# An expert's scatter at the end of the next expert, and each expert's count read at its own branch

## The reference

```python
def _moe_swiglu(h, w_router, b_router, w_gate, w_up, w_down):
    ...
    gates = jnp.einsum("tk,tke->te", top_w,
                       jax.nn.one_hot(top_idx, N_EXPERTS, dtype=jnp.float32))
    out = jnp.zeros((bsz * s, d), jnp.float32)
    for e in range(N_EXPERTS):
        y_e = _swiglu(tok, w_gate[e], w_up[e], w_down[e]).astype(jnp.float32)
        out = out + gates[:, e:e + 1] * y_e
    return out.astype(h.dtype).reshape(bsz, s, d)
```

## Time and profile before

| | us |
|---|---|
| median of 3 runs | 1776.54 (1773.34 to 1780.08) |
| profiled execution, its own time | 1776.94 |
| span of that execution's trace | 1775.1 |
| experts, first product of e0 to last product of e7 (from the timeline) | 837.85 to 1761.4 |
| PE busy over the span | 1599.4 (90%) |
| DMA, mean over the span | 274 GB/s, 403 to 409 GB/s in its fullest slices |

### The profile page before, as it was taken

The page is one execution under the profiler, slowest core; times in us unless marked ns, Lnnn a source line. Parts: engine busy times, 40 slices in busy tenths (PEclk is TensorE's granted clock), DMA queues, the critical chain, the costliest instruction groups (busy, mean ns, idle before and its releaser), DMA issues.

```text
span 1775.1 us, 24622 instructions
## 1 busy us (share of the span) xinstructions
PE 1599.4 (90%) x10871; PEld 912.8 (51%) x10872; DVE 371.6 (21%) x782; ACT 217.9 (12%) x416; POOL 101.7 (6%) x131
## 2 busy tenths in 40 slices
PE   7967899999999999997989999979979979887875
PEld 5633467777578866546343343345645653423322
DVE  1669320000055533403011001011011011110101
ACT  1411120000041133302000000000000000000001
POOL 5036200000000011100000000000000000000000
PEclk8988899999999999997999999999989989999999
DMA  9444576554384412332999977999969979999996
GB/s 330 150 147 167 189 279 250 220 218 150 113 311 143 143 48 75 116 142 96 382 403 409 362 290 267 404 408 408 403 250 347 388 266 397 403 409 404 409 408 248
DMA packets 167300, 485.81 MB, mean 274 GB/s; under 512 B 12928, under 2 KB 15872, under 8 KB 167168
## 3 DMA queue, kind: packets, MB, share of 16 engines
q1 hardware_dynamic: 157328, 481.51, 71.3%
q10 hardware_dynamic: 9840, 2.33, 0.7%
HBM read 482.78 MB, written 1.05 MB: 273 GB/s over the span
## 4 chain that ended last, share of the span: by engine, by line
PE 72%; DMA 11%; DVE 6%; issue 5%; SPq 2%; ACTq 1%; ACT 1%; POOL 0%; DVEq 0%
PE bank L1659 22%; PE bank L1209 20%; PE bank L1690 10%; DMA ring<-in_moe_w_down 8%; PE bank L1393 4%; PE bank L1584 3%; PE bank L1503 3%; DMA ring<-in_moe_w_up 3%; SPq L424 2%; PE bank L1636 2%; ACTq L530 1%; PE bank L1234 1%; DVE arena L921 1%; DVE arena L929 1%; PE bank L1542 1%
## 5 line engine op out<-in xcount | busy, mean ns | idle before, releaser
L1659 PE MATMUL bank<-ring,arena 128*32 128x256 f32 (+3 forms) x4864 | 510.0, 430 | 73.6 <-issue 46.6
L1659 PEld LDWEIGHTS bank<-ring,arena 128*32 128x32 f32 (+1 forms) x4864 | 230.1, 122 | 342.3 <-issue 267.7
L1209 PE MATMUL bank<-arena,ring 128*128 128x256 f32 x1280 | 287.0, 384 | 1.3 <-ACT arena L641 1.0
L1690 PE MATMUL bank<-ring,arena 128*32 128x256 f32 (+1 forms) x2128 | 253.2, 464 | 26.9 <-DMA ring<-in_moe_w_down 26.8
L1209 PEld LDWEIGHTS bank<-arena,ring 128*128 128x128 f32 x1280 | 243.9, 193 | 39.1 <-issue 4.5
L1690 PEld LDWEIGHTS bank<-ring,arena 128*32 128x32 f32 (+1 forms) x2128 | 103.1, 121 | 166.6 <-issue 119.6
L1134 DVE TENSOR_TENSOR arena<-arena,bank 128x512 f32<-128x512 f32 (+2 forms) x44 | 24.4, 576 | 607.8 <-PE bank L1659 607.8
L750 ACT ACTIVATE arena<-bank 128x512 f32<-128x512 f32 (+2 forms) x44 | 21.1, 508 | 696.7 <-PE bank L1671 576.4
L1393 PE MATMUL bank<-ring,arena 128*128 128x512 f32 x176 | 77.0, 595 | 0.3 <-PE bank L1209 0.3
L1234 PE MATMUL bank<-ring,cT 128*32 128x512 f32 x384 | 54.7, 695 | 8.9 <-ACT cT L583 8.3
L1503 PE MATMUL bank<-ring,arena 128*128 128x512 f32 x128 | 57.7, 593 | 0.3 <-PE bank L1209 0.3
(11 more groups left out here) (266 smaller groups left out, 1157.1 us busy)
## 6 DMA issues: line engine op xcount, KB each, us to landing
ring<-in_moe_w_gate SPq DMA_DIRECT2D x56, 2048.0 KB, 16.9
ring<-in_moe_w_up SPq DMA_DIRECT2D x56, 2048.0 KB, 16.8
ring<-in_moe_w_down SPq DMA_DIRECT2D x56, 2048.0 KB, 18.5
ring<-in_ada_w SPq DMA_DIRECT2D x24, 2048.0 KB, 9.1
ring<-in_m_w_in SPq DMA_DIRECT2D x12, 2048.0 KB, 9.1
ring<-in_ffn_w_gate SPq DMA_DIRECT2D x5, 2048.0 KB, 17.7
ring<-in_ffn_w_up SPq DMA_DIRECT2D x5, 2048.0 KB, 11.9
ring<-in_ffn_w_down SPq DMA_DIRECT2D x5, 2048.0 KB, 9.1
```

The lines of the kernel that those rows point to most:

```text
L1209: ins = mm(out_, l, r, start=i == 0, stop=i == len(pairs) - 1, **kw)
L1659: ins = mm(ps[base + b // per][m * h:m * h + m, w * (b % per):w * (b % per) + w], hcur3[:, kc, m * b:m * b + m], sl[:, kc - half * rows, w ...
L1690: ins = mm(ps[4 + b // per][m * h:m * h + m, w * (b % per):w * (b % per) + w], actT[:, t % 2, b // per, n * (b % per) + i, m * q:m * q + m ...
```

## The change

An expert's scatter moves. In experts 1 to 6 PE now runs `scatter(e-1)` as the very last thing of expert e's copy, right ahead of the jump or compare that leads to e+1. It writes banks 6, 7, 2, 3 instead of 6, 7, 4, 5 (`SCATTER_LATE`). DVE adds its result at the start of expert e+1, and PE waits for that before the first up tile of e+1. The last expert, e7, does it as before for e6: the scatter of e6 stands behind e7's first gate, with the old banks. Since y_sb of e-1 now lives until the end of e, ACT and DVE wait for `scat_mm` before they overwrite it, and there are three gate buffers instead of two (the third is part of `hd`).

`gather(0, 0)` and the eight idle products behind it move into e0's branch. Each engine loads an expert's count right ahead of that expert's branch, one load at each of eight places, instead of nine loads ahead of e0; the overflow flag is loaded at the end.

```diff
-        gates_of = (dtw.rearrange("p a b -> p (a b)"), area(3840, TOK))
+        gates_of = (dtw.rearrange("p a b -> p (a b)"), area(3840, TOK),
+                    hd.rearrange("p a b c -> p (a b c)")[:, 0:TOK])
...
-        SCATTER = (6, 7, 4, 5)
+        SCATTER, SCATTER_LATE = (6, 7, 4, 5), (6, 7, 2, 3)
...
                 act.wait_ge(s["tile_used"], k * ITEM + (MOE0 + ITEM))
+                past(act, "scat_mm", k * 4)
                 for dst, src in output_parts(nb, m, 0):
...
             def take_outputs(k, nb, m):
                 dve.wait_ge(s["tile_used"], k * ITEM + (MOE0 + ITEM))
+                past(dve, "scat_mm", k * 4)
...
             def item(e, nb, m):
 
-                if e:
-                    add_outputs(e - 1)
+                if e == NE - 1:
+                    add_outputs(e - 2, SCATTER_LATE)
+                    add_outputs(e - 1, SCATTER)
+                elif e >= 2:
+                    add_outputs(e - 2, SCATTER_LATE)
...
-                    take_gates(e + 1, gates_of[(e + 1) % 2], e)
+                    take_gates(e + 1, gates_of[(e + 1) % 3], max(e - 1, 0))
...
             gather(0, 0)
-            sizes = [count_of(dve, i) for i in range(NE)]
+            for e in range(NE):
+                sized(dve, count_of(dve, e), lambda nb, m: item(e, nb, m))
+            add_outputs(NE - 1, SCATTER)
             over = count_of(dve, 2 * NE)
-            for e in range(NE):
-                sized(dve, sizes[e], lambda nb, m: item(e, nb, m))
-            add_outputs(NE - 1)
...
             def item(e, nb, m):
-                expert(e, e, nb, m, lambda: scatter(e - 1, gates_of[(e - 1) % 2]) if e else None,
-                       lambda: gather(e + 1, e + 1) if e + 1 < NE else None)
+                last = e == NE - 1
+
+                def after_gate():
+                    past(pe, "acc_done", max(e - 1, 0) * 4)
+                    if last:
+                        scatter(e - 1, gates_of[(e - 1) % 3], SCATTER)
+
+                if e == 0:
+                    gather(0, 0)
+                    stay_warm(WARM_ITEM, 2)
+                expert(e, e, nb, m, e if last else max(e - 1, 0), after_gate,
+                       lambda: None if last else gather(e + 1, e + 1))
+                if e and not last:
+                    past(pe, "gT_ready", e + 2)
+                    scatter(e - 1, gates_of[(e - 1) % 3], SCATTER_LATE)
...
-            gather(0, 0)
-            stay_warm(WARM_ITEM, 2)
-            sizes = [count_of(pe, i) for i in range(NE)]
+            for e in range(NE):
+                sized(pe, count_of(pe, e), lambda nb, m: item(e, nb, m))
+            scatter(NE - 1, gates_of[(NE - 1) % 3], SCATTER)
             over = count_of(pe, 2 * NE)
-            for e in range(NE):
-                sized(pe, sizes[e], lambda nb, m: item(e, nb, m))
-            scatter(NE - 1, gates_of[(NE - 1) % 2])
```

More of the change, by code:

```diff
@@ L759, in _ @@
             first_counts(act, "act")
-            sizes = [count_of(act, i) for i in range(NE)]
+            for e in range(NE):
+                sized(act, count_of(act, e), lambda nb, m: item(e, e, nb, m))
             over = count_of(act, 2 * NE)
-            for e in range(NE):
-                sized(act, sizes[e], lambda nb, m: item(e, e, nb, m))
             items = overflow(act, "act", over, lambda: None, lambda g, k: item(g, k, 2, 64), lambda g, k: None)
@@ L1122, in take_tokens, with take_gates @@
                 ins.then_inc(s["hg_ready"], 1)
-            def take_gates(n, gates, k):
+            def take_gates(n, gates, scattered):
                 past(dve, "gT_mm", n + 1)
-                past(dve, "scat_mm", k * 4)
+                past(dve, "scat_mm", scattered * 4)
                 v.tensor_copy(gates, ps[3][:, 0:TOK]).then_inc(s["gT_ready"], 1)
@@ L1141, in take_outputs, with add_outputs @@
                 ins.then_inc(s["y_high"], 1)
-            def add_outputs(k):
+            def add_outputs(k, banks):
                 past(dve, "acc_done", k * 4)
@@ L1147, in add_outputs @@
                     past(dve, "scat_mm", k * 4 + i + 1)
-                    tt(o, o, ps[SCATTER[i]][:, :], ALU.add).then_inc(s["acc_done"], 1)
+                    tt(o, o, ps[banks[i]][:, :], ALU.add).then_inc(s["acc_done"], 1)
             def item(e, nb, m):
-                if e:
-                    add_outputs(e - 1)
+                if e == NE - 1:
[3 more added lines that the diff above has]
+                    add_outputs(e - 2, SCATTER_LATE)
                 for t in range(4):
@@ L1171, in more @@
                 take_outputs(k, 2, 64)
-                add_outputs(k)
+                add_outputs(k, SCATTER)
                 gather(g + 1, k + 1)
@@ L1629, in gather, with scatter @@
                 ins.then_inc(s["gT_mm"], 1)
-            def scatter(k, gates):
+            def scatter(k, gates, banks):
                 past(pe, "y_low", k + 1)
@@ L1667, in turn_hidden @@
                     if t == 0:
[L1668 removed]
+                        past(pe, "acc_done", added * 4)
                     for b, w in enumerate(bank_columns(nb, m, WIDTHS[t])):
@@ L1681, in output @@
                         past(pe, "y_high", k)
-                        past(pe, "acc_done", k * 4)
+                        past(pe, "acc_done", added * 4)
                     for row in range(parts * n):
@@ L1715, in item @@
             def item(e, nb, m):
-                expert(e, e, nb, m, lambda: scatter(e - 1, gates_of[(e - 1) % 2]) if e else None,
-                       lambda: gather(e + 1, e + 1) if e + 1 < NE else None)
+                last = e == NE - 1
[11 more added lines that the diff above has]
+                    scatter(e - 1, gates_of[(e - 1) % 3], SCATTER_LATE)
             def more(g, k):
-                expert(g, k, 2, 64, lambda: None, lambda: None)
-                scatter(k, gates_of[0])
+                expert(g, k, 2, 64, k, lambda: None, lambda: None)
+                scatter(k, gates_of[0], SCATTER)
                 gather(g + 1, k + 1)
```

5 lines of the change are left out of this document (2 added, 3 removed).

## The result

The changed kernel takes 1768.78 us (median of 6 runs, 1763.17 to 1770.16) against 1777.67 for the kernel before (6 runs beside it). The ratio is 0.9946, with a 95% interval of 0.9927 to 0.9965: 9.6 us faster by the ratio, 0.54%, of which the interval leaves 6 to 13; the medians are 8.9 apart. The forecast was 1765.5, with a range of 1757 to 1776.

What follows compares the result with a forecast made beforehand. The prediction took the end as set by PE work and DMA restarts at experts 0, 2 and 5, then by the DMA alone. Gains of 4.8 + 2.0 + 4.65 = 11.4 from 1776.94 gave 1765.5 us, range 1757 to 1776.

Steps and rivals of the forecast that it cites:

- the three restarts: First tiles used by experts 0, 2 and 5, where the DMA restarts; gains of 4.8, 2.0 and 4.65 us.
- Branches as fetches: Unexplained PE idle at expert jumps, 2.71 to 9.51 us, is instruction fetch, 3.5 to about 6 us a page.
- First restart: At expert 0: gather waits for the fetch, gate follows at full clock, first tile used at 839.8; gain 4.8 us.
- Second restart: At expert 2: idle 2.8 to 4.1 instead of 4.29; gain 2.0 us, the middle between clock falling and holding.
- Third restart: From expert 2's end to expert 5's gate: shorter idle at the jumps, one more scatter; gain 4.65 us.
- the fetch of 10.4: Ahead of expert 4: two jumps cost two fetches of 5.2 us, 9.51 idle plus 0.9 covered by queued records.
- The lead of 16 records: PE's sequencer reaches a jump with 16 records queued; a scatter there adds 1.9 or 3.2 us of cover.
- DVE and the tail: DVE's adds (4 x 0.7 us) finish before PE asks for them, and the tail is unchanged: no cost.
- Third scatter: From expert 2's end to expert 5's gate three scatters stand instead of two, costing 3.6 us.
- The load that waits for an empty PE: Rival: no fetch is covered at any jump from expert 2 on; 1785 us, slower; chance 0.08.
- The rival that the fetches stretch by what the scatter covers: At the second and third restarts the added 1.9 and 3.2 us covers vanish; 1776 us, no change; chance 0.23.

Runs made afterwards that it cites:

- e2: Not a run: expert 2 of the kernel's eight; PE's idle ahead of it was 4.29 us in the kernel before, 5.49 in the changed kernel.
- e3: Not a run: expert 3 of the kernel's eight, a 3x32 copy here; PE's idle ahead of it was 2.71 us before, 1.12 in the changed kernel.
- e5: Not a run: expert 5 of the kernel's eight; PE's idle ahead of it was 9.30 us in the kernel before, 7.07 in the changed kernel.
- late_in_3x32: Kernel before with counts loaded at the branches and the scatter late in 3x32 copies only, first gather ahead of the first branch: 1764.28 us, ratio 0.9939.
- scatter_late_only: Changed kernel with the nine loads and the first gather ahead of the first branch again, so only the scatter has moved: 1769.98 us, ratio 0.9965 to before.
- Held refill: Changed kernel, but SP refills an expert's last tile's slot only after the next expert's first tile has been used: one run, 1775.08 us.
- extra4: Changed kernel with four idle 128x512 products (8 records) added behind each late scatter, ahead of the jump: single run 1768.76 us.
- branch-free pair: Kernel before and changed kernel, each without size branches and count loads, the copies these inputs take in a row: 1730.59 and 1732.86 us.
- loads_at_branch: Kernel before with each expert's count loaded right ahead of its branch, gather and scatter left in place: 1770.55 us, ratio 0.9963.
- gather_in_branch: Kernel before with the loads at the branches and the first gather and its idle products inside the first branch: 1771.41 us, ratio 0.9975.
- the three shifted ones: Changed kernel, kernel before and late_in_3x32 with 100, 53 and 53 never-run PE instructions in expert 1's 3x32 copy: ratios 0.9914, 0.9966, 0.9914 to before.

## Why the prediction was right, and where its steps were not

The time and the sign hold, and the three restarts account for 5.8 of the profile's 7.1. The second of them went the other way, though, and the third gave half of its forecast; the range was wide enough for both. The tally of the steps, in the changed kernel:

- **Branches as fetches.** Right, and shown: without branches and loads every such idle time is gone, 45 us in all. The Trainium skill has the rule in "Runtime: NRT & Kernel Launch", Instruction fetch mechanics: a taken branch whose target is outside the sequencer's window forces a fetch by DMA; the trace agrees.
- **First restart**, forecast 4.8, measured 4.6 (839.98, forecast 839.8). Right in its steps too: the gather's end was forecast for 834.1 and came at 834.4, the gate's start for 836.3 and came there. What the sum did not tell apart are the two parts: the loads' move is worth 5.4 alone, and the gather's takes 0.9 back. The load itself, taken as 0.35, is 0.305 to 0.34. The Trainium skill, in the same section of "Runtime: NRT & Kernel Launch", gives about 0.2 us a register for the loads that the runtime puts ahead of a kernel; here a load took half as much again or more.
- **Second restart**, forecast +2.0, measured -1.1: SP's refill on e2's first tile went out at 1093.9 before, 271.2 behind the counts, and at 1090.3 after, 267.7, 3.5 earlier where 4.6 had been in hand. This is the step that failed. The clock fell as it had before (0.50 in the stretch from 1083), where I had taken the middle between falling and holding, but the larger part is the fetch. I had named the refill under the fetches and let it cost at most 1.4, for an idle time of 4.1 at the most; it was 5.49. By an estimate with a lead of 26 records and 0.3 for the load, the two fetches at e2 took 12.8, against 10.0 before and 9.4 with the refill held back.
- **Third restart.** Idle ahead of e3 1.12 (forecast 1.15), a stop after 42 records (43) of 2.92 (3.3), stops in piece 3 of e3 5.07 together (5.8, for four page ends; there were three), in e4's 3.59 (2.7). Ahead of e4 8.15 instead of 6.7 and ahead of e5 7.07 instead of 6.5. Together 2.3 instead of 4.65 from e2's end to e5's gate, of which the idle at e4 is the largest part. The term that was off is the fetch of 10.4: it was 1.5 longer there. It is not the cover that failed: with the same late scatter the idle ahead of e4 was 6.63 in late_in_3x32, as forecast for the changed kernel, and 6.76 in scatter_late_only, which has no load there. Held refill takes 1.8 off the 8.15, so the DMA has a share; for the rest see below.
- **The lead of 16 records.** Too short: an estimated 24 to 28. The savings of 3.2 and 1.9 a jump need only eight; extra4 shows 3.19 at e5, 2.82 at e4 and 1.37 at e2.
- **DVE and the tail.** Right. DVE's adds ran from 1079.89 to 1082.4, ahead of even the gate of e2, and from the last PE row to the end of the span it is 12.8 us in both.
- **Third scatter.** I charged 3.6 for it up to e5's gate. In the branch-free pair it costs 3.7 up to there, and 0.7 at the end.
- **Rivals.** The load that waits for an empty PE is refuted by loads_at_branch. The rival that the fetches stretch by what the scatter covers held at e2, and in part at e4: the true course lies between it and my forecast, and so does the measured time.

The sum of the three restarts, 4.6 - 1.1 + 2.3, is 5.8; the stretches between and behind them gave 1.2, for which the forecast had no term, and that makes the 7.1 of the profile. The forecast of 11.4 was thus too high by the second restart (3.1) and the third (2.3), most of it the idle ahead of e4 (1.5). The 9.6 of the ratio lies between 7.1 and 11.4; that the median came within 3.3 of the forecast is in part luck, as the sum that gave it was 4.3 too high for the profiled pair. Whether the change is faster by more than half a per cent is not settled by an interval of 0.35% to 0.73%.

**What stays open.** By the same estimate, with a lead of 26 records, the two fetches to e4 come to 10.8 to 11.0 in the kernels whose jump lies, by count, about 170 of 256 instructions into its page (before, loads_at_branch, late_in_3x32), to 11.4 in scatter_late_only (181), 11.5 in gather_in_branch (113), 12.5 in the changed kernel (124) and 13.3 to 13.6 in the three shifted ones (224). The place in the page matters, but the order of these numbers fits no simple rule, and what makes the fetch long was not measured by itself.

## What to carry to other kernels

A branch to code that is not yet fetched costs a fetch, and the engine shows only the part of it that its queued work does not cover. That cover was so many records here, so slow records right ahead of the jump help, and a large DMA that starts under the fetch hurts. Where a stretch of very short instructions stops every so many records, count instructions to the next page end: in the kernel before, padding that never runs was worth more than half of the whole reordering. Split a change of three parts, and compare the parts by repeated times as well as by single traces: here one part lost time at the place where it acts, and traces and times disagree on what two of the parts bring.

## What the runs showed of the hardware that I had not expected

- The queue ahead of PE held more than 16 records (weight load and product), an estimated 24 to 28, by idle times of 7.07, 3.88 and 0.51 ahead of e5 as the number of slow records ahead of the jump went from 8 to 16 to 32.
- The same two fetches left 5.49 us in view with the weight DMA at 1.05 and 0.58 of its capacity, and 2.14 with the refill held back and the DMA at 0.06 and 0.05.
- A register load takes 0.305 to 0.34 us (2.44 and 2.72 for eight on ACT), and PE's sequencer passes it with work still queued: the idle times ahead of e2, e4 and e5 grew by 0.15 to 0.5 with a load ahead of each jump.
- 53 instructions of padding that are never executed made the kernel before 0.34% faster (0.21% to 0.46%).
